# Routing one fetched tile first with its U rows multiplied in the routing stage, a sent table at position five, and a dense stage with split operands

## The reference

```
h = einsum('thkd,td->thk', u[e], tb)
a = gelu(h) * g
out = einsum('thk,thkd->td', a, v[e])
```

## Time and profile before

| | |
|---|---|
| median of three runs | 3752.91 us (3752.08 to 3759.64) |
| profiled execution, its own time | 3756.75 us |
| its span | 3755.0 us |
| busy: PE, DVE, ACT, POOL | 91%, 71%, 24%, 39% |
| mean granted clock of PE | 0.958 |
| moved by DMA | 1201 MB, 320 GB/s over the span |
| `decide` | about 960 to 1903 us |
| `dense` | 1903 to 3755 us |

### The profile page before, as it was taken

The page is one execution under the profiler, slowest core; times in us unless marked ns, Lnnn a source line. Parts: engine busy times, 40 slices in busy tenths (PEclk is TensorE's granted clock), DMA queues, the critical chain, the costliest instruction groups (busy, mean ns, idle before and its releaser), DMA issues.

```text
span 3755.0 us, 45250 instructions
## 1 busy us (share of the span) xinstructions
PE 3435.2 (91%) x14374; PEld 2026.9 (54%) x14374; DVE 2662.5 (71%) x4988; ACT 890.0 (24%) x1844; POOL 1447.1 (39%) x1116
## 2 busy tenths in 40 slices
PE   8998989986889998999549999999999999999998
PEld 7444879884466667677414444444444444444443
DVE  0453887756368755655768888887888888889786
ACT  1452211215122338797100000100001000100001
POOL 0000187740232778874023343333343334333331
PEclk8899999988899999999779999999999999999999
DMA  7898499975887668888679999999999999999994
GB/s 262 342 421 298 136 401 378 378 275 168 322 311 252 170 179 182 193 147 190 205 285 398 406 398 390 398 390 391 409 385 400 406 397 418 401 399 365 387 379 185
DMA packets 470727, 1201.16 MB, mean 320 GB/s; under 512 B 196953, under 2 KB 261897, under 8 KB 391817
## 3 DMA queue, kind: packets, MB, share of 16 engines
q0 software_dynamic: 149776, 679.68, 47.7%
q1 hardware_dynamic: 187200, 498.50, 35.7%
q10 hardware_dynamic: 133568, 20.84, 3.5%
HBM read 1127.33 MB, written 72.61 MB: 320 GB/s over the span
## 4 chain that ended last, share of the span: by engine, by line
PE 32%; DVE 8%; issue 4%; DMA 4%; DVEq 1%; POOL 1%; POOLq 0%
PE d_ps L2482 17%; PE d_ps L2471 15%; DVE d_acc L2367 4%; DMA d_ring<-peer_uv,d_idx 3%; DVE d_ring L2353 3%; DMA out_y<-k_yacc 1%; DVE d_qacc L2384 1%; DVE k_yacc L2367 1%; POOL d_ring L2315 0%; DVE d_aw L2362 0%; DVE d_a L2375 0%; DVE d_qacc L2413 0%; DVEq L2362 0%; DVEq L2353 0%; DVEq L2366 0%
## 5 line engine op out<-in xcount | busy, mean ns | idle before, releaser
L2315 POOL DMA_INDIRECT d_ring<-peer_uv,d_idx x512 | 654.3, 1278 | 1067.1 <-DVEq L2369 964.1
L2471 PE MATMUL d_ps<-k_xd,k_ring 128*128 128x512 f32 x2048 | 907.0, 596 | 74.6 <-SPq L2283 60.4
L2471 PEld LDWEIGHTS d_ps<-k_xd,k_ring 128*128 128x128 f32 x2048 | 391.5, 191 | 569.4 <-issue 508.3
L2353 DVE SCALAR_TENSOR_TENSOR d_ring<-d_ring,k_xn 128x1024 f32<-128x1024 f32 x512 | 605.6, 1219 | 70.2 <-DMA d_ring<-peer_uv,d_idx 39.5
L2482 PE MATMUL d_ps<-d_v,d_a 128*128 128x512 f32 x1024 | 456.9, 600 | 32.5 <-DVE d_a L2375 24.6
L2482 PE MATMUL d_ps<-k_ring,d_a 128*128 128x512 f32 x1024 | 451.7, 594 | 16.1 <-DVE d_a L2375 16.1
L1630 POOL DMA_INDIRECT G<-c_cellg,c_cell x256 | 420.2, 1641 | 116.8 <-issue 90.1
L2367 DVE SCALAR_TENSOR_TENSOR d_acc<-d_ring,d_aw,d_acc 128x1024 f32<-128x1024 f32 x256 | 328.8, 1284 | 49.9 <-DVE d_acc L2367 32.3
L2367 DVE SCALAR_TENSOR_TENSOR k_yacc<-d_ring,d_aw,k_yacc 128x1024 f32<-128x1024 f32 x256 | 328.7, 1284 | 47.8 <-DVE k_yacc L2367 31.7
L2482 PEld LDWEIGHTS d_ps<-d_v,d_a 128*128 128x128 f32 x1024 | 196.3, 193 | 284.7 <-issue 283.4
L2438 ACT ACTIVATE d_ge<-d_h (+1 forms) x256 | 52.1, 203 | 1238.6 <-DVE d_ring L2353 1238.5
(11 more groups left out here) (382 smaller groups left out, 4442.3 us busy)
## 6 DMA issues: line engine op xcount, KB each, us to landing
c_chunk<-wq SPq DMA_DIRECT2D x128, 512.0 KB
k_ring<-u_blocks SPq DMA_DIRECT2D x128, 512.0 KB, 12.7
s_kc<-sb_kT SPq DMA_DIRECT2D x32, 1024.0 KB, 9.1
s_vc<-sb_v SPq DMA_DIRECT2D x32, 1024.0 KB, 7.3
c_chunk<-w_m SPq DMA_DIRECT2D x64, 512.0 KB
k_ring<-v_blocks SPq DMA_DIRECT2D x64, 512.0 KB, 13.4
d_gb<-G SPq DMA_DIRECT2D x32, 1024.0 KB
d_v<-v_blocks SPq DMA_DIRECT2D x64, 512.0 KB
```

Source lines behind the costliest of these rows:

```text
L2315: pool.indirect_dma_start(out=ring[:, b], out_offset=None, in_=a["peer_uv"], in_offset=bass.IndirectOffsetOnAxis(ap=idx8[par][:, b:b + 1], ...
L2353: last = nc.vector.scalar_tensor_tensor(ring[:, b, 0:D], ring[:, b, 0:D], 1.0, xn[T % 2][:], ALU.mult, ALU.mult, accum_out=h[:, bass.ds(co ...
L2471: last = nc.tensor.matmul(ps[:, HB + x % 2, :], ub[j][:, k], xd[:, k].rearrange("p t q -> p (t q)"), start=(k == 0), stop=(k == KC - 1))
```

## The change

In `decide` the order of the kinds becomes: position 1 fetched, 2 sent, 3 and 4 hot, 5 sent, 6 to 8 fetched (`TILE` maps the places in memory to tiles). The indices of position 1 give `row0`, and POOL gathers its 128 rows of u, 4 KB each, with three buffers (`early_rows`); DVE multiplies them with the kept `xn0` (`dots`), 16, 20, 19, 21 and 10 of them spread evenly over the `between()` points of iterations 4 to 8, and 6, 12, 12 and 12 beside the products of `experts_of` in iterations 5 to 8. POOL's list puts these gathers at fixed places among the scatters. The buffers come from the one-hot chunks: `DEEP` goes from 6 to 3. The 56 rows for the samples are fetched earlier, in iterations 2 and 3.

In `dense` position 1 needs only its v rows, a gather of half the size, and the three other fetched tiles go side by side, four gathers per block, with two buffers for each of the three and one for the v rows. `hidden` splits u and x into a high part in float32r and the rest: u_high with x_high and x_low, u_low with x_high, 24 matmuls in float32r per block in place of 8 in float32. ACT copies the high part of u, DVE subtracts for the low part (`low`, 128x1024). Half of the sums of `values` stay in PSUM from the first block to the last, so DVE takes one result per block and not two.

```diff
-    MADE = ... + [[0, 2, 2, 1, 1, 1], [0, 1, 1, 1, 1, 1, 1], [0, 1, 1, 1, 1, 1, 1, 1]]
-    BEFORE, WITHIN, AFTER = {6: 3, 7: 1, 8: 1}, {6: 12, 7: 12, 8: 9}, {6: 3, 7: 3}
-    QUAD, DEEP, TS = 4, 6, 32
+    MADE = ... + [[0, 2, 1, 1, 1, 1], [0, 2, 1, 1, 1, 1, 1], [0, 2, 1, 1, 1, 1, 1, 1]]
+    BEFORE, WITHIN, AFTER = {6: 1}, {6: 12, 7: 12, 8: 12}, {6: 3, 7: 3}
+    BETWEEN, DOTS, DOTS_BESIDE = 29, {4: 16, 5: 20, 6: 19, 7: 21, 8: 10}, {5: 1, 6: 2, 7: 2, 8: 2}
+    EB, EARLY_AT = 3, 3
+    QUAD, DEEP, TS = 4, 3, 32
+    SENT, HOTS = (2, 5), (3, 4)
...
+                def early_rows(n):
+                    for k in range(asked[0], min(asked[0] + n, P)):
+                        if k >= EB:
+                            pool.wait_ge(dotted, k - EB + 1)
+                        pool.indirect_dma_start(out=ring[:, EARLY_AT + k % EB], ..., in_=rows,
+                                                in_offset=...row0[:, k:k + 1]...).then_inc(filled[EARLY_AT + k % EB], 16)
+                        asked[0] = k + 1
+                pool.wait_ge(rows_ready, 1)
+                pool.wait_ge(summed, REST)
+                early_rows(DOTS[4] + EB)
...
                     for s in range(16 * h, 16 * h + 16):
                         pool.indirect_dma_start(out=grid, ..., compute_op=ALU.add).then_inc(scattered[q], 16)
-                for h in range(4):
-                    scatter_head(0, h)
-                for h in range(4):
-                    scatter_head(1, h)
-                    scatter_head(0, h + 4)
-                for h in range(4):
-                    scatter_head(1, h + 4)
+                        if s % rows_after[0] in rows_after[1]:
+                            early_rows(1)
+                for h in range(8):
+                    scatter_head(0, h, (5, (0, 2, 4)))
+                for h in range(8):
+                    if h == 0:
+                        early_rows(10)
+                    scatter_head(1, h, (2, (1,)))
+                early_rows(P)
...
+                def dots(n):
+                    for k in range(dots_done[0], dots_done[0] + n):
+                        s = EARLY_AT + k % EB
+                        dve.wait_ge(filled[s], 16 * (len(range(s, REST, RB)) + k // EB + 1))
+                        nc.vector.scalar_tensor_tensor(ring[:, s], ring[:, s], 1.0, xn0[:], ..., accum_out=h0[:, k:k + 1]).then_inc(dotted, 1)
...
                         if passed[0] % 4 == 1 and n <= t:
                             logs(t, n)
                             one_hots(MADE[i][n])
...
+                        due = DOTS.get(i, 0)
+                        dots(due * passed[0] // BETWEEN - due * (passed[0] - 1) // BETWEEN)
```

More of the change, by code:

```diff
@@ L58 @@
 REST = 56
+TILE = (1, 4, 2, 3, 0, 5, 6, 7)
 CLEARED = 64
@@ L2295, in _ @@
-                group(1, 1, sums)
-                with sp.Fori(1, NG // 2) as i:
+                gates(0, 0)
+                for T in range(FETCHED):
+                    sp.dma_start(acc[T][:], o["ys"][DENSE + T]).then_inc(acc_in, 16)
+                gates(0, 1)
+                group(0, 0, beside=sums)
+                group(1, 1)
+                with sp.Fori(1, NG // 2 - 1) as i:
                     for u in range(2):
                         group(2 * i + u, u)
+                group(NG - 2, 0)
@@ L2343, in _ @@
+                body(0)
+                with pool.Fori(1, P // BODY) as k:
+                    body(k)
             @block.vector
@@ new lines, in add_rows @@
+                def add_rows(k, x):
+                    b = BODY * k + x
+                    first = number(k) and x == 0
+                    dve.wait_ge(row_gelu, b + 1)
+                    nc.vector.tensor_tensor(aw[:, x, :, None], ge[:, x, :, None], gw[:, 1:, bass.ds(b, 1)], ALU.mult).then_inc(weighed, 1)
+                    dve.wait_ge(weighed, b + 1)
+                    if first and k == 0:
+                        dve.wait_ge(acc_in, 16 * FETCHED)
+                        dve.wait_ge(early_weighed, 1)
+                    for T in range(LOADED):
+                        if not (first and k == 0):
+                            dve.wait_ge(added[1 - x % 2][T], 4 * k + (x + 1) // 2)
+                        nc.vector.scalar_tensor_tensor(acc[T + 1][:], both[x % 2][T][:, D:], aw[:, x, T:T + 1], acc[T + 1][:], ALU.mult, ALU.add).then_inc(added[x % 2][T], 1)
+                    dve.wait_ge(filled0, 16 * (b + 1))
+                    if not (first and k == 0):
+                        dve.wait_ge(added0, b)
+                    nc.vector.scalar_tensor_tensor(acc[0][:], values0[:], h0[:, bass.ds(b, 1)], acc[0][:], ALU.mult, ALU.add).then_inc(added0, 1)
@@ L2386, in body @@
-                def body(T, k):
-                    start = 0 if number(k) else T * TB // BODY
+                    nc.vector.tensor_tensor(part, ps[:, VB + c % 2, :], part, ALU.add).then_inc(v_taken, 1)
+                def body(k):
                     for x in range(BODY):
@@ new lines, in _ @@
+                for half in range(2):
+                    part = slice(half * KC // 2, (half + 1) * KC // 2)
+                    dve.wait_ge(x_high_done, half + 1)
+                    nc.vector.tensor_tensor(x_low[:, part], x_all[:, part], x_high[:, part].bitcast(F32), ALU.subtract).then_inc(x_low_done, 1)
+                dve.wait_ge(early_gelu, 1)
+                nc.vector.tensor_tensor(h0[:], h0[:], gw[:, 0], ALU.mult).then_inc(early_weighed, 1)
+                body(0)
+                with dve.Fori(1, P // BODY) as k:
+                    body(k)
@@ L2454, in square_sum @@
                     act.wait_ge(rms, 2 * n + 1)
                     nc.scalar.activation(small[:, n, 1:2], small[:, n, 0:1], ACT.Sqrt, scale=1.0 / D, bias=eps[:]).then_inc(rms, 1)
-                def tile_done(T):
-                    square_sum(T, acc[T % 2][:], summed, P * (T + 1))
-                bodies(act, body, tile_done)
+                for half in range(2):
+                    part = slice(half * KC // 2, (half + 1) * KC // 2)
+                    nc.scalar.activation(x_high[:, part], x_all[:, part], ACT.Copy).then_inc(x_high_done, 1)
@@ new lines, in _ @@
+                nc.scalar.activation(h0[:], h0[:], ACT.Gelu).then_inc(early_gelu, 1)
+                act.wait_ge(eps_done, 2)
+                act.wait_ge(x_low_done, 2)
+                body(0)
+                with act.Fori(1, P // BODY) as k:
+                    body(k)
+                for T in range(FETCHED):
+                    if T:
+                        act.wait_ge(added[1][T - 1], P // 2)
+                    else:
+                        act.wait_ge(added0, P)
+                    square_sum(T, acc[T][:])
```

452 lines of the change are left out of this document (232 added, 220 removed).

## The result

The changed kernel takes 3903.57 us (median of four runs, 3887.5 to 3906.12), the kernel before 3752.49 in the same session: a ratio of 1.039 [1.0358, 1.0422], 3.9% slower. Forecast were 3795 and a range of 3680 to 3890. The sign was right, the size outside the range. The profiled execution has a span of 3899.6 us against 3755.0, 144.6 more.

What follows compares the result with a forecast made beforehand. The prediction took PE and DMA both to bound the kernel, with DVE's waits on the path in `decide`. `decide` +200 us and `dense` -158 gave +42: 3799 profiled, 3795 median, range 3680 to 3890.

Steps and rivals of the forecast that it cites:

- Dense: In `dense`, DMA bounds at 12.6 us per block, period 12.7 with PE at 12.15; 158 us less kept.
- the margin of 1.5%: In `dense`, the old period's excess over the larger of its two (13.95 to 13.75), used in taking 12.7 us.
- Rival B: In `dense`, late gathers end each block 0.7 us late, 13.4 us; gain only 68 us, total 3885; chance 0.12.
- 1. up to position 2's weights: In `decide`, iterations 2 to 4: moved sample rows, four each in iterations 3 and 4, fall into the attention, +8 us.
- Term 2: In `decide`, iterations 5 and 6: DVE's dots wait for rows POOL brings every 5.1 us, +25 and +34 us.
- my own upper bound: In `decide`, iterations 5 and 6: all of the rows' delivery time reaches the path, 90 us.
- Term 3: In `decide`, iterations 7 and 8: with DEEP 3, DVE waits 6.2 us per step for PE's spread; with dots, +45 and +55.
- Term 4: At the end of `decide`, POOL's second scatter, after position 5's weights, ends 34 us after DVE; `dense` starts 200 us later.
- Rival C: In `decide`, iterations 7 and 8: PE falls to half clock while waiting, up to +69 us, total 3864; chance 0.12.
- Rival A: In `decide`, routing absorbs the rows: only DVE's extra attention work counts, +90 us, total 3685; chance 0.26.

Runs made afterwards that it cites:

- e2_norows: The changed kernel without the 128 gathers of early rows, all dots still made, on buffer contents times zero: 3733.36 us.
- e1_made: The changed kernel with one one-hot chunk of iterations 7 and 8 made ahead of the attention instead of in its step 1: 3820.71 us.
- e8_order: e1_made with only POOL's list changed, early rows closer at first and thinner later in both scatters: 3794.38 us.
- e12_plan3: e8_order's three row and five chunk buffers, with POOL's list worked out from the dots' times in e6_made_norows: 3769.04 us.
- The square of runs: The changed kernel, e1_made (earlier chunks), e2_norows (no early-row gathers) and e6_made_norows (both edits): 3903.57, 3820.71, 3733.36 and 3672.24 us.
- e6_made_norows: The changed kernel with both edits, one-hot chunks made earlier and no gathers of early rows: 3672.24 us.
- e15_half_scatter: The changed kernel with 64 instead of 128 scatters of position 5's weights, half of that tile's table left out: 3829.27 us.
- e11_plan4: e1_made with four row and four chunk buffers, and POOL's list worked out from the dots' times in e6_made_norows: 3753.56 us.
- e13_move6: e11_plan4 with six dots moved from iteration 8 to iteration 4 and POOL's list worked out again: 3760.32 us.
- e14_move12: e11_plan4 with twelve dots moved from iteration 8 to iteration 4 and POOL's list worked out again: 3761.46 us.
- e7_nodots: e6_made_norows with each dot of early rows cut from 1024 columns to 64: 3640.66 us.

## Why the prediction was wrong, step by step

**Dense: right.** 12.7 us per block, measured 12.81; 158 us of gain, measured 152. DMA runs at 386 to 389 GB/s, not 395. Two details of the working do not hold: 13.75, from which the margin of 1.5% comes, follows from none of its rows (the larger of PE's 13.6 and DMA's own 13.95 gives 2.6% or nothing), so 12.7 is close in part by luck; and PE stands at 97.5%, not under 97. The 418 of the best stretch before was not held. Nor were the 436 GB/s of the Trainium skill, "DMA: Bandwidth & Descriptors", section "Anatomy of one DMA"; here the measurement decides. PE's 12.15 us is 12.3. Rival B's 13.4 is excluded, though DVE does wait 252 us for gathers in the whole stage, six times as long as before: its slack pays for it, and little of that is left, since it is also busy for 426 of 500 us.

**Decide: each term is there, each is too small, and the sum is 97 us too small.** Growth from weights to weights, against the forecast:

| term | forecast | measured |
|---|---|---|
| 1. up to position 2's weights | 8 | 16 |
| 2. iteration 5 | 25 | 51 |
| 2. iteration 6 | 34 | 40 |
| 3. iteration 7 | 45 | 58 |
| 3. iteration 8 | 55 | 70 |
| position 6's to position 8's weights | 0 | -2 |
| 4. DVE's end to the start of dense | 34 | 63 |
| sum | 200 (rounded) | 297 (rounded) |

Term 2, the step that failed most: 91 us against 59. I had POOL's rate about right (5.1 us per row; it issued one per 5.3 and 5.5 us in iterations 5 and 6, its waits for dots taken off), and the failed step is how much of the delivery time reaches the path. Of the 59 us, 20 were DVE's own extra work, which left 39 for the waits after slack and margins. Without rows the two iterations grow by 9 us (e2_norows): the work costs less than I had. The supply costs the other 83. DVE waits 101 us for rows there, and its slack took only 18 of them; 91 is about my own upper bound, all of the delivery time. I took one side only: POOL brings rows too slowly in the attention. It also reaches rows whose dots are not yet due and stands there with its scatters behind it, 183 us from its first scatter on. These scatters are late in the next phase, in which rows wait behind them, 7 to 9 us after their buffer came free. A list with fixed places loses at both ends, and the orders show what that is worth: e1_made, e8_order and e12_plan3 have the same instructions and the same buffers, at 3821, 3794 and 3769.

Term 3, 128 us against 100. 13 waits of 6.2 us were forecast, 81 us; there are 18 with 105.9 us. Thirteen of them are those of the forecast, 99.8 us or 7.7 each: the count is right and the length is not. This is what one looks like, in step with the earlier trace rows:

```profile
1697.90 2.88 PE L2126 MATMUL c_ps<-k_ring,c_negtri 128*128 128x512 f32 x4
...
1700.62 1.88 PE L2130 MATMUL c_ps<-c_past,c_negone 128*128 128x512 f32 x4
...
1702.34 1.05 PE L2089 MATMUL c_ps<-k_ring 128*128 128x128 f32 x8
...
1703.43 0.69 DVE L1855 TENSOR_TENSOR k_ring<-c_iota,c_turned 128x512 f32<-128x512 f32 x1 [7.59 <-PE c_ps L2089]
1704.04 1.22 DVE L1842 SCALAR_TENSOR_TENSOR k_ring<-k_ring,c_xn 128x1024 f32<-128x1024 f32 x1
```

The mechanism is the predicted one: DVE stands until the spread of this same step is over, then makes its dot. PE's part of it has grown. The four matmuls of L2126 take 2.88 us here and 3.78 in a step of iteration 8, at a mean granted clock of 0.74 (1695 to 1704 us) and 0.66 (1891 to 1901 us). In the step of the earlier trace rows, at a clock of 1.00, the kernel before has them in 1.98:

```profile
1673.19 1.98 PE L2083 MATMUL c_ps<-c_soft,c_negtri 128*128 128x512 f32 x4
```

So here the lower clock lies within DVE's wait. The waits are 1.5 us longer than forecast, 13 times, so it is worth up to 20 us there, by an estimate. The square of runs splits the 128 us by iterations 7 and 8 of the table: without rows the buffer wait takes 87 of them (e2_norows less e6_made_norows), everything else but rows 25 (e6_made_norows less before), the rows 17. Against the forecast's 60, 25 and 15 it is the buffer wait that was mis-sized, and not the rows. That e1_made gained 83 us, close to the 85 forecast, is chance: the 85 hold 25 us of dots, which e1_made still makes.

Term 4, 63 us against 34. DVE waits 66 us for POOL's end. From position 5's weights to the last scatter's start it takes from 1806 to 2194, 388 us and not 345. POOL's last row, behind which the last scatters stand, is issued 207 us after position 5's weights, and not the forecast 175: POOL stands 84 us at rows whose dots are not made, all in iteration 8, which takes 217 us and not the forecast 202. DVE's own end comes 14 us later than forecast from the same point, and the difference is the 29. e15_half_scatter confirms the term as such.

**Rival C was no alternative but a part of the truth.** I gave half clock 0.12 and only iterations 7 and 8. From position 2's to position 6's weights, first the changed kernel, then e6_made_norows, which has no rows to wait for and 19 us of buffer waits:

```profile
1271.00:2023.00 752.00, 552.86 (x3467) 401.90 (x3480) 431.06 (x1228) 378.69 (x755) 452.93 (x285) 0.86 0.74 198
```

```profile
1264.00:1830.00 566.00, 499.93 (x3468) 363.18 (x3468) 427.12 (x1229) 377.46 (x753) 348.50 (x192) 0.98 0.69 160
```

PE does the same matmuls in 553 us of busy time instead of 500 (494 at a clock of 0.99 in the kernel before). A mean of 0.86 between levels of 1 and 0.5 is, by an estimate, 28% of the stretch, 210 us, at 1.2 GHz; in e6_made_norows it is 4%. The clock is lowest where PE waits most: 0.75 from 1615 to 1710 us, in which PE is busy for 55 of 95 us. The Trainium skill, "TensorE: Matmul & The Clock Gate", section "HAM oscillation", says so of matmuls with a wait in each round, and the trace agrees. These 53 us of busy time are inside the growth of all terms; up to 20 of them lie within term 3's waits and so on the path, and how much of the rest does, no run separates.

**Rival A** (3685) needed terms 2 and 3 under 95 us; they are 220. Its idea is true of the arithmetic: e6_made_norows, with all dots and no supply, is 3672, without what its missing gathers would load. The error was not in the list of mechanisms. It was in their sizes: slack that hid little (term 2), buffer waits priced at full clock (part of term 3), and an iteration 8 that holds POOL's rows back (term 4).

## What to carry to other kernels

Where one queue serves two consumers by a fixed order (here gathers for DVE and scatters for memory), read both waits, the consumer's and the queue's: if both are large, the order is wrong, and a list worked out from the consumer's own times is worth more than a buffer (25 us with three buffers and 44 with four; the fourth buffer nothing before it, and 15 after). A transfer stage's gain must be weighed against what its early part takes from a stage that is a chain. And terms that put waits into a chain through PE should be priced with PE's busy time at the lower clock too.

## What was not expected

141 us of dots moved the time by only 32, on a DVE that was busy for 427 of 566 us. Four-byte scatters cost POOL their issue, 1.55 to 1.58 us at the median and 0.3 between two, in every kernel. With the landing at each head (14 waits, 47.8 us in e11_plan4) position 5's 128 took 304 to 312 us where POOL waited for dots 0.6 to 15 us (e11_plan4, e13_move6, e14_move12), and 282 to 298 us without any row (e2_norows, e6_made_norows, e7_nodots); that floor follows position 5's weights, wherever they come. No version that does all of the work beats the kernel before: the best, e11_plan4, stands at 0.9997, because what `dense` gives (152 us) is then what `decide` takes.
